# A fused mLSTM / sliding-window decoder trunk on one core: sums on another engine, a split moved one item later, and a new order where the first run begins

## The reference, cut to what matters

```
def swiglu(x, w_gate_up, w_down):
    gu = x @ w_gate_up
    g, u = jnp.split(gu, 2, axis=-1)
    return (jax.nn.silu(g) * u) @ w_down

def mlstm_mixer(...):
    ...
    h = h * lax.rsqrt(jnp.mean(h * h, axis=-1, keepdims=True) + EPS)
    h = h * head_norm.astype(jnp.float32).reshape(NH_A, DV_A)
    h = h.reshape(Bsz, S, V_W) * jax.nn.sigmoid(o.astype(jnp.float32))
    return h.astype(x.dtype) @ w_out

for l in range(DEPTH):
    x = x + mixer_l(rmsnorm(x, norm_l))          # mlstm_mixer, then swa_sink_mixer
    x = x + swiglu(rmsnorm(x, ffn_norm[l]), w_gate_up[l], w_down[l])
```

## Time and profile before

| | us |
|---|---|
| median of 3 timed runs | 2181.03 (2179.17 to 2181.78) |
| profiled execution, its own time | 2173.61 |
| span of the profiled execution | 2171.8 |
| PE busy in the span | 2066.7 (95%) |
| DVE / POOL / ACT busy | 1350.0 / 1240.3 / 936.1 |
| mean granted PE clock | 0.983 of full speed |

### The profile page before, as it was taken

One profiled execution on the slowest core, in us unless ns is written; L12 is line 12 of the kernel. 1 busy time (PEld: TensorE's weight loads), 2 busy tenths in 40 slices (PEclk: granted clock), 3 DMA queues, 4 the chain that ended last, 5 costly groups with the idle time before them and its releaser, 6 DMA issues.

```text
span 2171.8 us, 29514 instructions
## 1 busy us (share of the span) xinstructions
PE 2066.7 (95%) x10032; PEld 1710.3 (79%) x10032; DVE 1350.0 (62%) x2104; ACT 936.1 (43%) x1997; POOL 1240.3 (57%) x1075
## 2 busy tenths in 40 slices
PE   7899999888999999999998999898899999999997
PEld 6788988777877877888876777687788887888885
DVE  7663552666767766464664776757676675645566
ACT  5444333264544544332353544435445444432233
POOL 4542421557877887565657000155888886846565
PEclk9999999999999999999998999999999999999999
DMA  5655536644667777795723000463467676678672
GB/s 137 204 193 180 170 145 221 243 126 130 226 233 245 244 222 231 267 367 189 251 91 86 21 20 21 176 219 101 144 224 235 220 245 213 214 300 319 204 260 108
DMA packets 295432, 415.04 MB, mean 191 GB/s; under 512 B 40040, under 2 KB 218232, under 8 KB 295296
## 3 DMA queue, kind: packets, MB, share of 16 engines
q1 hardware_dynamic: 260752, 307.87, 43.1%
q10 hardware_dynamic: 33120, 100.68, 13.0%
q0 software_dynamic: 1424, 4.77, 0.6%
HBM read 259.09 MB, written 154.17 MB: 190 GB/s over the span
## 4 chain that ended last, share of the span: by engine, by line
PE 74%; DVE 7%; DMA 5%; POOL 5%; ACT 4%; issue 4%; SPq 1%; ACTq 0%; POOLq 0%; DVEq 0%
PE ps L2080 18%; PE ps L2082 17%; PE ps L2081 17%; PE ps L1983 7%; PE ps L1985 3%; DMA scratch_forms<-prep_forms 3%; PE ps L2308 2%; POOL sum_a L953 1%; PE ps L2205 1%; PE ps L2206 1%; PE ps L2202 1%; PE ps L2343 1%; PE ps L2345 1%; POOL X L1115 1%; PE ps L2135 1%
## 5 line engine op out<-in xcount | busy, mean ns | idle before, releaser
L2080 PE MATMUL ps<-forms,mats 128*128 128x512 f32 x2016 | 794.6, 394 | 54.5 <-DVE X L1566 16.5
L2082 PE MATMUL ps<-forms,mats 128*128 128x512 f32 x2016 | 789.6, 392 | 0.0
L2081 PE MATMUL ps<-forms,mats 128*128 128x512 f32 x2016 | 789.4, 392 | 0.0
L963 POOL TENSOR_TENSOR mats<-sum_a,mats 128x256 fp32r<-128x256 f32 (+2 forms) x392 | 414.3, 1061 | 420.9 <-ACT mats L1181 420.0
L2080 PEld LDWEIGHTS ps<-forms,mats 128*128 128x128 f32 x2016 | 381.8, 189 | 148.0 <-issue 55.4
L2082 PEld LDWEIGHTS ps<-forms,mats 128*128 128x128 f32 x2016 | 381.2, 189 | 80.0
L2081 PEld LDWEIGHTS ps<-forms,mats 128*128 128x128 f32 x2016 | 381.5, 189 | 78.0
L1566 DVE TENSOR_TENSOR X<-ps,X 128x512 f32<-128x512 f32 x390 | 267.1, 689 | 210.6 <-PE ps L2082 208.0
L1181 ACT ACTIVATE mats<-sum_a 128x256 fp32r<-128x256 f32 (+2 forms) x392 | 201.3, 516 | 322.5 <-PE ps L2082 285.6
L1545 DVE TENSOR_TENSOR mats<-stream_raw,mats 128x256 fp32r<-128x256 f32 (+2 forms) x300 | 277.2, 925 | 48.7 <-ACT mats L1181 47.8
L1181 ACT ACTIVATE mats<-stream_raw 128x256 fp32r<-128x256 f32 (+2 forms) x302 | 156.6, 519 | 262.7 <-PE ps L2082 255.9
(11 more groups left out here) (214 smaller groups left out, 2819.0 us busy)
## 6 DMA issues: line engine op xcount, KB each, us to landing
forms<-scratch_forms ACTq DMA_DIRECT2D x182, 512.0 KB, 5.3
scratch_forms<-prep_forms SPq DMA_DIRECT2D x161, 512.0 KB, 3.5
stream_raw<-in_w_gate_up_dram SPq DMA_DIRECT2D x88, 512.0 KB, 5.6
scratch_forms<-head_forms SPq DMA_DIRECT2D x49, 512.0 KB, 2.6
scratch_hidden<-hidden SPq DMA_DIRECT2D x84, 256.0 KB, 5.6
prep_raw<-in_w_down_dram SPq DMA_DIRECT2D x38, 512.0 KB, 5.5
stream_raw<-scratch_hidden SPq DMA_DIRECT2D x32, 512.0 KB, 4.7
forms<-scratch_forms SPq DMA_DIRECT2D x28, 512.0 KB, 8.7
```

Of the source, the lines that this page charges most:

```text
L963: pool.tensor_tensor(blocks(m[:, q, 1, :], it.width), stream_source(it, q), blocks(m[:, q, 0, :].bitcast(F32), it.width), ALU.subtract).th ...
L2080: mm(dst, ah, bh, start=OPENS[q] and k == 0, stop=False, skip_group_check=True)
L2081: mm(dst, ah, bl, start=False, stop=False, skip_group_check=True)
L2082: m = mm(dst, al, bh, start=False, stop=k == w - 1, skip_group_check=True)
```

## The change: two parts at item 8 and three at the beginning of the first run

1. In each run, the four stream sums of item 9 are made by DVE at the end of item 7 (they were made by POOL), and DVE makes all low parts of item 9 (POOL made four of the seven).
2. Step 7 of the forms of x: its two sums stay at product 5 of item 8, but the four high parts (ACT) and four low parts (DVE) move to products 1 and 2 of item 9.
3. SP loads item 3 before x tile 7 and the four stores, no longer behind them.
4. `scale_head` of the last head is ahead of item 0 on DVE, with the last low part of item 0 between its two steps.
5. ACT makes the third of the four sigmoids one step earlier, and PE waits for the fourth (bank 3) only at item 1.

```diff
-        XF_STEPS_AT = {0: 5, 3: 6, 5: 7}
+        XF_STEPS_AT = {0: 5, 3: 6}
+        LAST_STEP_AT = {1: (2,), 2: (3, 0, 1)}
...
-                    if l == 0 and i == 0:
+                    if l == 0 and i == 1:
                         sp.wait_ge(d_add, NQ)
                         load_x(7)
...
 # POOL
-                            if (q2 == 1) if its[i + 1].plain else (q2 in SUM_A):
+                            if (q2 == 1) if its[i + 1].plain else (q2 in SUM_A and not it.plain):
                                 stream_lo(its[i + 1], q2)
...
-                    elif i + 2 < len(its):
-                        if i == 7:
-                            pool.wait_ge(xf_lo_dve, xf_no_dve(l, 3, 1))
+                    elif i + 2 < len(its) and i != 7:
                         stream_sums(its[i + 2])
...
 # ACT
+                        if i == 9:
+                            for g in LAST_STEP_AT.get(q, ()):
+                                x_form_hi(l, 7, g)
...
+                    if last and c == 7:
+                        gate_sigmoid(1, 0)
                     act.wait_ge(bank_free[b], Ks[b] + i // 4 + 1)
                     act.activation(hjunk[:], H[:, c, :], ACT.Square, accum_out=hsq[:, 0, c:c + 1]
...
 # DVE
+            def stream_sums(it):
+                w = it.width
+                dve.wait_ge(stream_loaded[stream_buffer(it)], stream_arrived[it.n])
+                dve.wait_ge(loS, 4 * it.n)
+                a11, a12, a21, a22 = (stream_view(it, j) for j in range(4))
+                s = [blocks(t[:], w) for t in sums_a[w]]
+                dve.tensor_tensor(s[0], a21, a22, ALU.add).then_inc(ssum, 5)
+                dve.tensor_tensor(s[2], a11, a21, ALU.subtract)
+                dve.wait_ge(ssum, 4 * it.n + 1)
+                dve.tensor_tensor(s[1], s[0], a11, ALU.subtract).then_inc(ssum, 2)
+                dve.wait_ge(ssum, 4 * it.n + 3)
+                dve.tensor_tensor(s[3], a12, s[1], ALU.subtract).then_inc(ssum, 1)
...
-                        if it.n == 0 and q == 1:
-                            scale_head(NH_A - 1)
...
+                        if it.plain and q == 5:
+                            x_form_sums(l, 7, (0, 1))
...
+                        if i == 9:
+                            x_form_lo(l, 7, LAST_STEP_AT.get(q, ()))
...
                         x_form_lo(l, 4, QUARTERS)
+                        stream_sums(its[9])
...
-            stream_lo(items[0], 6)
+            scale_head(NH_A - 1, between=6)
             run(0)
...
 # PE
-                for b in range(4):
+                for b in range(3):
                     pe.wait_ge(bank_free[b], uses.before[b])
                 for it in its:
+                    if local(it) == 1:
+                        pe.wait_ge(bank_free[3], uses.before[3])
```

More of the change, by code:

```diff
@@ L1410, in head, with gate_sigmoid @@
                 Ks = uses.stage(STATE)
+                def gate_sigmoid(j, half):
+                    b_o = 2 * j + half
+                    act.wait_ge(bank_full[b_o], Ko[j][b_o] + 1)
+                    if half == 0 and not first:
+                        act.wait_ge(y_stored[j], 32 * h)
+                    act.activation(yh[:, j, half * 512:(half + 1) * 512],
+                                   ps[:, b_o, :], ACT.Sigmoid).then_inc(bank_free[b_o], 1)
                 for c in range(TT):
@@ L1428, in head @@
                         j = c // 4
-                        for half in range(2):
-                            b_o = 2 * j + half
-                            act.wait_ge(bank_full[b_o], Ko[j][b_o] + 1)
-                            if half == 0 and not first:
-                                act.wait_ge(y_stored[j], 32 * h)
-                            act.activation(yh[:, j, half * 512:(half + 1) * 512],
-                                           ps[:, b_o, :], ACT.Sigmoid).then_inc(bank_free[b_o], 1)
+                        for half in range(int(last and c == 7), 2):
+                            gate_sigmoid(j, half)
             head(0, 0, True)
@@ L1666, in run @@
                         for q2 in refill_after(it, q):
-                            if (q2 != 1) if its[i + 1].plain else (q2 in PLAIN_A):
+                            if (q2 != 1) if its[i + 1].plain else (q2 in PLAIN_A or it.plain):
                                 stream_lo(its[i + 1], q2)
@@ L1761, in scale_head @@
                                   ).then_inc(hms_ready, 1)
+                if between is not None:
+                    stream_lo(items[0], between)
                 dve.wait_ge(hrs_ready, h + 1)
```

5 lines of the change are left out of this document (3 added, 2 removed).

## The result

The changed kernel takes 2167.48 us (median of 8 runs, 2165.02 to 2171.68) where the kernel before took 2180.1 in the same comparison (8 runs; one stray run of 2836 us is among them and does not move the median). The ratio is 0.9944, 95% interval 0.9928 to 0.9960: 12.6 us faster, by the interval 9 to 16. Forecast were 20.4 us less, 2160.6, range 2154 to 2171. Sign and range held; the size was off by 7, and the range held because it had been drawn wide enough for two rivals that came true in part.

The account below looks back on a forecast made before the run. PE, busy 95% of the span, was taken as the bound, so only its waits counted. Gains 6.4 + 7.5 + 5.5 + 1.0 = 20.4 us, subtracted from the median 2181.0, gave 2160.6; the 8-in-10 range was 2154 to 2171.

Parts of the forecast that it names:

- Start (parts 4 and 5): Beginning of run 0: earlier sigmoid and head scaling gain 1.0 us, bounds 0 and 1.5; the wait moves to DVE's first addition.
- Transfers (part 3): Run 0, item 2: the 4.14 gap goes with 1.7 of slow matmuls, less 0.3 for item 4; gain 5.5 us.
- the 0.3 for item 4: Loss taken in item 3 of run 0 because item 4's load waits for the stores: 0.3 us, bounds 0 and 4.
- R2: Rival: the late transfer moves to item 4, PE waits 4 in item 3 and loses 1.7 after; 2166.0 us, chance 0.10.
- Items: Item 9: loss of 10.7 in run 0 and 11.8 in run 1 falls to 4.3 each; gains 6.4 and 7.5 us.
- the one of 2.3: PE's wait before product 2 of item 9, forecast to stay at 2.3 us, bounds 1.5 and 4.
- The 5.96: PE's idle time before product 2 of item 9, run 0, in the kernel before; put down to POOL's late first sum.
- The term of 1.0 for POOL's sums of item 10: Item 9, product 6 waiting for the last of step 7 and two additions: 1.0 us lost per run, bounds 0 and 3.
- R1: Rival: contention moves, POOL's item 10 sums are held and products 4 and 6 of item 9 wait; 2168.8 us, chance 0.14.
- R3: Rival: DVE becomes the bound before and in item 9, 31 instructions at 1.45 us each; 2205 us, slower, chance 0.05.
- The term of 1.0 for slow matmuls: Item 9, slow matmuls after the gap that stays: 1.0 us lost per run, bounds 0 and 3.1.
- R4: Rival: later PE gaps grow by what is won; 2181 with all returned, 2171 with half; chance 0.13.

Follow-up runs that it names:

- experiment 5: Changed kernel with the transfers in the old order: tile 7 and the four stores ahead of item 3's load; 2167.18 us, ratio 0.9950 against the kernel before.
- experiment 7: Changed kernel with the load of x tile 7 behind the four stores instead of ahead of them; 2161.74 us, ratio 0.9928 against the kernel before.
- experiment 10: Changed kernel with item 10's sums on DVE too and tile 7's load behind the stores; 2153.43 us, ratio 0.9884 against the kernel before.
- experiment 11: Changed kernel with the four stores ahead of item 3's load and x tile 7 behind both; 2165.64 us, ratio 0.9929 against the kernel before.
- experiment 3: Kernel before plus only item 9's sums and low parts on DVE, step 7 staying in item 8; 2171.93 us, ratio 0.9980 against the kernel before.
- experiment 4: Kernel before plus only step 7's move to item 9, item 9's sums staying on POOL; 2171.31 us, ratio 0.9971 against the kernel before.
- experiment 1: Kernel before plus parts 1 and 2 alone (items 8 and 9), start and transfers as before; 2168.75 us, ratio 0.9953 against the kernel before.
- experiment 2: Kernel before plus parts 3, 4 and 5 alone (beginning of run 0), items 7 to 9 as before; 2173.67 us, ratio 0.9981 against the kernel before.
- experiment 8: Changed kernel with the first two preparation loads held until item 9's last product is done; 2165.42 us, ratio 0.9938 against the kernel before.

## Why the prediction was right in sign and too large

**Start (parts 4 and 5), forecast 1.0.** Right in kind and too small: PE's first product is 1.3 earlier (means of five profiles each, 373.60 and 372.34), the wait for the addition is 2.21 instead of the forecast 3.3, and product 4 starts at 383.60 where 384.7 was forecast. Over all profiles it starts 2.8 earlier (mean 385.45 in the five with the old start, 382.68 in the nine with the new). Chance has a share in such a figure: in four of the nine profiles 11.2 to 11.3 us pass from the first product to product 4, in the other five 9.7. In the changed kernel, one of the four, matmuls at 0.43 start to start stand behind the wait of 2.21. The forecast let DVE's scaling end at 378.4; it ended at 376.8:

```profile
374.52 2.29 DVE L1790 TENSOR_TENSOR h_head<-h_head,h_sumsq 128x2048 f32<-128x2048 f32 x1 [1.05 <-POOL h_sumsq L1068]
```

**Transfers (part 3), forecast 5.5: failed.** The term that failed is the 0.3 for item 4: PE waited 5.00 there, which is the rival R2, given 0.10. Three readings were off, and they add up to it. First, "PE would reach product 4 of item 3 at 415.1": it was there at 412.44 (417.44 less the wait), 2.7 earlier. The 415.1 is 409.73 - 4.14 + 7 x 1.36, the old kernel's time, without the gain at the start that the same prediction forecast. Second, the load was to be issued by 408 and was at 408.85, 0.8 later; the stores landed only that much behind the forecast 406 to 408. Third, ACT had the load 6.2 us after its issue (415.04), where 4.6 was taken, 1.6 later. Measured against 412.44, the load had to land by 410.0 and so to be issued by 405.4: stores that landed at 408 would have left a wait of about 2.6 even so.

The argument "the same bytes pass" was nearly right and did not go far enough. It says when the last transfer ends, not which one is last, and 512 KB of tile 7 stayed ahead of what was wanted first. Experiments 5, 7, 10 and 11 show it: with item 3's load before or behind, no gain is seen; with tile 7 at the end item 7 starts at 461 to 462, where it was 469.0 before, more than the 6.5 forecast for the whole start. Start and transfers together gained 1.5 at item 7 (468.98 on average in the five profiles with the old start and order, 467.50 in the five with the new): the start's 2.8 less about 1.3 that the new order took. The single profiles spread by 5 us, so neither figure is sharp.

**Items, forecast 6.4 and 7.5.** The forecast waits were right: the gaps forecast to go went, the one of 2.3 came as 1.88. The cause was right for the gap of 2.27 only. The 5.96 was put down to the late sum too, and experiments 3 and 4 show that it hangs on the place of step 7 on ACT; both parts stood in the change, so the forecast did not suffer. The term of 1.0 for POOL's sums of item 10 was mis-sized: 2.60. Rival R1 had named it, and the argument against R1 ("POOL gets its turn after two or three instructions") looked at the wrong side. POOL did get its turn; it was DVE that slowed, to 1.84 for the first low part and 1.45 for each of the other three. The row of 5.81 for four had shown that price, and I used it only as the bound of another term. R3, DVE at such a pace all through, did not come: up to item 9's last low part DVE kept 0.60 from start to start, with POOL idle until 510.23. The page "SBUF — State Buffer" of the Trainium skill, section "Who interferes with whom", has the two engines lock each other out by whole instructions. Where both have work queued, the trace agrees in kind: the DVE instructions take up to 1.78 instead of 0.68 and POOL's 1.7 (3.45 for two) instead of the 1.29 that it needs alone. For the 10.05 row it does not.

The term of 1.0 for slow matmuls is a coin toss. Of ten gaps of 2.6 (changed kernel, experiments 1, 5, 7 and 11, two runs each), five were followed by matmuls at 0.43 start to start instead of 0.23. Windows of the two kinds, the changed kernel first, then experiment 1, each with its gap in it:

```profile
1544.00:1550.00 6.00, 3.42 (x12) 2.65 (x12) 3.19 (x5) 2.31 (x4) 3.45 (x4) 0.85 0.64 229
```

```profile
1550.00:1556.00 6.00, 3.43 (x15) 2.53 (x15) 4.35 (x6) 2.30 (x4) 3.59 (x3) 1.00 0.44 156
```

After the same wait the granted clock falls to its lower level (1.2 GHz) in the one and stays at 2.4 GHz in the other. The fall costs 1.6 us: run 1's lead over before in item 10 is 4.5 where it fell and 6.1 where it didn't.

**Given back (R4).** Small. Run 1's lead is 5.5 on average in item 10 (4.5, 6.1, 6.1, 4.5, 6.1 in those five kernels) and 4.1 at item 29, so 1.4 goes back. In run 0 the spread of the kernel before alone is 6.7, so nothing can be read there from two profiles.

**The sum in the traces.** 1.5 up to item 7; run 0 3.5 (440.8, the mean of before twice and experiment 2, less 437.3, the mean of the five kernels); run 1 4.1 (434.0 less 429.9). Together 9.1, where the times say 12.6 (9 to 16). Against the forecast 20.4 the traces lack 5.0 up to item 7 (6.5 forecast, 1.5 found), 3.4 in run 1 (2.0 in item 9, of which 1.6 before product 6, and 1.4 given back) and 2.9 in run 0, where the same 1.6 before product 6 is seen and the rest can't be split. Which waits behind item 10 give back the 1.4 stays open; that the first loads of the preparation do not pace them is shown (experiment 8). With the two misses that are explained put into the forecast's own sum, 5.4 for R2 and 1.6 in each run, it would have read 2169.2; measured were 2167.48.

## What to carry to other kernels

When a transfer is late, ask which one in the queue is wanted last, check by how much it may slip, and put that one last; exchanging two urgent ones only moves the wait. When a forecast moves PE forward in one place, move it forward in the next sum too, or the slack there comes out too large. When two engines that slow each other are pulled apart in one place, look at the next place where both have work, and charge the slowed price to the engine on the critical path. Before a difference between two profiles is explained, profile the unchanged kernel a second time: here two executions of it differed by 6.7 us in one stage.

## What the runs showed of the hardware

A POOL addition of 128x512 lasted 10.05 us beside DVE's uninterrupted series of instructions with both inputs in SBUF, and DVE lost nothing (0.60 from start to start). Alone such a POOL instruction takes 1.29 (median of the 54 that overlap no DVE instruction in the first profile of before). Once POOL's were already running back to back when DVE's came, both paid: POOL's took 1.29 to 1.75, DVE's up to 1.85 instead of 0.68. A store of 256 KB from SBUF landed, in the median of the four, after 5.7 us with nothing issued just ahead (experiment 11), after 8.1 to 11.1 with one load of 512 KB just ahead (tile 7 in the six profiles with the old order, item 3's load in experiments 7 and 10), and after 13.9 to 14.2 with both ahead (five profiles); in the last case one issue alone held SP for 5.1 us each time. And the granted clock, after ten waits of the same length in the same place, fell five times.
